# Two gates and the inner values of a linear-attention head: from head columns to token rows, gated before the transposition

## What is computed

```
proj = u @ w_in                  # (hq, hf, hi, hg, gq, gk, gv, ga, gb, gz, gate_h, gate_g)
o_h = hgrn2_chunked(silu(hq)*s, k_h, hi, log_f)           # 8 heads of 128
o_h = rmsnorm(o_h, hgrn_out_norm) * silu(hg)
y_h = o_h @ w_branch_hgrn
o_g = gated_delta_chunked(q_g, k_g, cv, beta, g)          # 16 value heads of 128, 8 key heads
o_g = rmsnorm(o_g, gdn_out_norm) * silu(gz)
y_g = o_g @ w_branch_gdn
y = sigmoid(gate_h) * y_h + sigmoid(gate_g) * y_g         # then y @ w_out
```

## Time and profile before

| | us |
|---|---|
| median of 3 runs | 1413.3 (1413.23 to 1413.37) |
| the profiled execution | 1413.49 |
| its span in the trace | 1411.8 |
| TensorE busy in the span | 1389.9 (98%) |
| VectorE busy | 1042.1 (74%) |
| ScalarE busy | 793.2 (56%) |

### The profile page before, as it was taken

How to read it: one execution, slowest core, us unless ns; L and a number is a source line. 1 busy time by engine, 2 the same in 40 slices (tenths; PEclk the granted TensorE clock), 3 DMA queues, 4 the chain that set the end, 5 groups by cost and what they waited for, 6 DMA issues and landing times.

```text
span 1411.8 us, 26224 instructions
## 1 busy us (share of the span) xinstructions
PE 1389.9 (98%) x9590; PEld 1276.0 (90%) x9590; DVE 1042.1 (74%) x1558; ACT 793.2 (56%) x1275; POOL 28.9 (2%) x73
## 2 busy tenths in 40 slices
PE   8999999999999999999999999999999999999998
PEld 8999999988888878888899999999999898888887
DVE  5786776677666686666798888888888857666665
ACT  4345454644343454444578788788788753544443
POOL 6000000000000000000000000000000000000000
PEclk9999999999999999999999999999999999999999
DMA  8465454565555646566664534534543256556661
GB/s 268 139 179 148 131 138 149 184 206 179 179 191 197 209 140 188 181 196 189 166 165 119 145 96 116 148 98 112 147 104 114 89 155 215 158 180 196 197 199 63
DMA packets 304639, 224.91 MB, mean 159 GB/s; under 512 B 10418, under 2 KB 288068, under 8 KB 304580
## 3 DMA queue, kind: packets, MB, share of 16 engines
q1 hardware_dynamic: 304580, 224.09, 53.7%
HBM read 223.02 MB, written 1.05 MB: 159 GB/s over the span
## 4 chain that ended last, share of the span: by engine, by line
PE 88%; DVE 7%; ACT 2%; DVEq 1%; issue 1%; DMA 0%; ACTq 0%
PE G L1794 10%; PE G L1796 10%; PE G L1795 10%; PE M L1809 7%; PE G L1809 7%; PE M L1799 5%; PE M L1800 5%; PE M L1801 5%; PE G L1811 4%; PE M L1811 4%; PE G L2440 2%; DVE w_lo L1049 2%; PE M L2275 1%; DVEq L1046 1%; PE M L1794 1%; PE G L2442 1%
## 5 line engine op out<-in xcount | busy, mean ns | idle before, releaser
L1049 DVE TENSOR_TENSOR w_lo<-w_raw,w_hi 128x2048 fp32r<-128x2048 f32 (+2 forms) x209 | 475.3, 2277 | 167.6 <-ACT w_hi L575 162.9
L575 ACT ACTIVATE w_hi<-w_raw 128x2048 fp32r<-128x2048 f32 x207 | 394.4, 1907 | 178.9 <-PE G L1796 76.4
L1794 PE MATMUL G<-xa,w_hi 128*128 128x256 f32 x1280 | 382.5, 299 | 0.0
L1796 PE MATMUL G<-xa,w_lo 128*128 128x256 f32 x1280 | 361.9, 283 | 0.0
L1795 PE MATMUL G<-xa,w_hi 128*128 128x256 f32 x1280 | 361.6, 282 | 0.0
L1794 PEld LDWEIGHTS G<-xa,w_hi 128*128 128x128 f32 x1280 | 244.5, 191 | 3.4 <-issue 3.2
L1795 PEld LDWEIGHTS G<-xa,w_hi 128*128 128x128 f32 x1280 | 244.7, 191 | 1.7 <-issue 1.7
L1796 PEld LDWEIGHTS G<-xa,w_lo 128*128 128x128 f32 x1280 | 244.0, 191 | 0.0
L1799 PE MATMUL M<-w_hi,xb 128*128 128x512 f32 x304 | 118.8, 391 | 0.1
L1800 PE MATMUL M<-w_lo,xb 128*128 128x512 f32 x304 | 118.7, 390 | 0.0
L1801 PE MATMUL M<-w_hi,xb 128*128 128x512 f32 x304 | 118.3, 389 | 0.0
(11 more groups left out here) (381 smaller groups left out, 2276.1 us busy)
## 6 DMA issues: line engine op xcount, KB each, us to landing
w_raw<-in_w_in SPq DMA_DIRECT2D x166, 512.0 KB, 4.7
w_raw<-in_ffn_w_in SPq DMA_DIRECT2D x88, 512.0 KB, 5.0
w_raw<-in_w_ff SPq DMA_DIRECT2D x64, 512.0 KB, 4.0
w_raw<-in_ffn_w_out SPq DMA_DIRECT2D x44, 512.0 KB, 4.6
w_raw<-in_w_out SPq DMA_DIRECT2D x16, 512.0 KB, 4.3
w_raw<-in_w_branch_gdn SPq DMA_DIRECT2D x16, 512.0 KB, 5.1
w_raw<-in_w_branch SPq DMA_DIRECT2D x12, 512.0 KB, 4.3
w_raw<-in_w_branch_hgrn SPq DMA_DIRECT2D x8, 512.0 KB, 4.0
```

Of the source, the lines that this page charges most:

```text
L575: nc.scalar.activation(w_hi[:, slot, :], w_raw[:, slot, :], ACT.Copy).then_inc(hi_ready, 1)
L1049: return v.tensor_tensor(dst, src, hi.bitcast(F32), ALU.subtract)
L1794: mm(out_, w[0], x[0], start=first, stop=False)
L1796: return mm(out_, w[1], x[0], start=False, stop=last_)
```

## The change

Chunks 4 and 5 of a head are laid out anew: each holds, for four of the eight k, 512 columns: 128 of hi, 128 of hg, 256 of gz. In their products the tokens are stationary and the weights move (`token_quarter`, with `three_x`), so 48 products of 512 columns take the place of 96 of 256. Tokens 0 to 127 gather in G's bank 1, tokens 128 to 255 in M0, and VectorE and ScalarE copy one each into `tok`. hi needs no transposition any more. One Silu covers hg and gz. The outputs are multiplied with 1/rms and gate by VectorE while tokens are on partitions (`hgrn_gate`, `delta_gate`), then transposed, and ScalarE takes them out with the gain. `level(0)` uses M1 instead of M0, and the transposed matrix M5 instead of M4. In pass 8 the low part of the first four heads' output comes before `scored(0)`, branch products start at place 1, the `WARM` products go, chunks are split in halves, and `delta_turned` follows tile 4.

The core of the diff:

```diff
-EV_Y = (EV_HEADS[0] + 3 * GH, EV_HEADS[1] + 3 * GH)
+EV_Y = (EV_HEADS[0] + 2 * GH, EV_HEADS[1] + 3 * GH)
...
+        def load_tok(c, slot, part, h):
+            slot_free(c)
+            k = slice(4 * part, 4 * part + 4)
+            for at, col in ((0, O_HI), (P, O_HG)):
+                sp.dma_start(rows4(w_raw, slot)[:, :, at:at + P], w_in2[:, k, ds(col + h * P, P)]).then_inc(w_loaded[slot], 16)
+            sp.dma_start(rows4(w_raw, slot)[:, :, T:2 * T], w_in2[:, k, ds(O_GZ + h * CW, CW)]).then_inc(w_loaded[slot], 16)
...
 ScalarE
-            def scaled(out_, o, total, rstd, scale):
+            def token_rstd(out_, o, total, rstd, scale):
...
-                nc.scalar.activation(rstd, rstd, ACT.Exp, scale=-0.5)
-                settle()
-                for x in range(n):
-                    ins = nc.scalar.activation(out_[:, x, :], o[:, x, :], ACT.Copy, scale=rstd[:, x:x + 1])
-                return ins
+                return nc.scalar.activation(rstd, rstd, ACT.Exp, scale=-0.5)
...
+            if not gemm:
+                o_hi(1, 0, 4)
             if main:
                 z_copy(1)
                 y_copy(0)
                 act.wait_ge(gemm_done, c0 + i * 6)
-                nc.scalar.activation(sgz, G[:, 0, :].rearrange("p (e t) -> p e t", e=2), ACT.Copy).then_inc(evac[0], 1)
+                nc.scalar.activation(tok[:, 1, :], M[:, 0, :], ACT.Copy).then_inc(tok_ready, 1)
...
+            if main and gemm:
+                act.wait_ge(hss_done, i)
+                nc.scalar.activation(o_h[:, ds(i - 1, 1), :].rearrange("p n t -> p (n t)"), M[:, 1, T:2 * T], ACT.Copy,
+                                     scale=vec[:, V_HN:V_HN + 1]).then_inc(hfin, 1)
...
 VectorE
+        def delta_gate(i):
+            dve.wait_ge(grs_ready, i)
+            for b in range(TT):
+                for e in range(2):
+                    x, at = 2 * b + e, T + P * e
+                    ins = v.scalar_tensor_tensor(out=zi[:, b, e, :], in0=M[:, 5, P * x:P * x + P], scalar=o_rstd[:, x:x + 1],
+                                                 in1=tok[:, b, at:at + P], op0=ALU.mult, op1=ALU.mult)
+            ins.then_inc(gsq_ready, 1)
...
             decayed(2)
+            if main and gemm:
+                w_low(c0 + 4 + RING - 6, i, 6)
+            if not gemm:
+                o_low(1, 0, 4)
             scored(0)
...
-            w_low_j(3)
             if main and gemm:
-                delta_out(i)
+                delta_gate(i)
...
                 v.drain().then_inc(y0_ready, 1)
+                if main:
+                    delta_out_low(i)
...
                 middle(2)
-            if main and gemm:
-                delta_out_low(i)
+            w_low_j(3)
             if gemm:
-                chunk_done(4)
-                v.tensor_copy(hvt, G[:, 1, 0:T])
-                v.tensor_copy(hsg, G[:, 1, T:2 * T]).then_inc(evac[1], 1)
-                settle()
-            w_low_j(4)
+                dve.wait_ge(tok_done, i + 1)
+                v.tensor_copy(tok[:, 0, :], G[:, 1, :]).then_inc(evac[1], 1)
             settle()
...
 TensorE
-        EARLY = {5: (0, 3), 6: (3, 4), 7: (4, 7), 8: (7, 9), 9: (9, 12), 10: (12, 14), 11: (14, 17), 12: (17, 19),
-                 13: (19, 21), 14: (21, 25), 15: (25, 28)}
-        WARM = {1: 1, 2: 2, 3: 2, 4: 2}
+        EARLY = {1: (0, 2), 2: (2, 3), 3: (3, 5), 4: (5, 6), 5: (6, 8), 7: (8, 10), 8: (10, 11), 9: (11, 13), 10: (13, 14),
+                 11: (14, 17), 12: (17, 19), 13: (19, 21), 14: (21, 25), 15: (25, 28)}
+            def token_quarter(n):
+                part, b, k0 = n // 4, n % 4 // 2, 2 * (n % 2)
+                if n % 4 == 0:
+                    weights_ready(c0 + 4 + part + i * 6)
+                if n == 0:
+                    pe.wait_ge(evac[1], EV_HEADS[1] + 2 + i * 3)
+                wh, wl = rows4(w_hi, (c0 + 4 + part) % RING), rows4(w_lo, (c0 + 4 + part) % RING)
+                blk = slice(P * b, P * b + P)
+                for k in range(k0, k0 + 2):
+                    x = 4 * part + k
+                    ins = three_x(G[:, 1, :] if b == 0 else M[:, 0, :], (xa_hi[:, x, blk], xa_lo[:, x, blk]),
+                                  (wh[:, k, :], wl[:, k, :]), x == 0, x == KT - 1)
+                if n % 4 == 3:
+                    ins.then_inc(gemm_done, 1)
+                if n == 5:
+                    ins.then_inc(tok_done, 1)
...
-            if gemm:
-                pe.wait_ge(evac[1], EV_HEADS[1] + 3 + i * 3)
-                for b in range(TT):
-                    ins = nc.tensor.transpose(M[:, 1, P * b:P * b + P], hvt[:, P * b:P * b + P], ident[:])
-                ins.then_inc(hvt_done, 1)
```

More of the change, by code:

```diff
@@ L192, in emit @@
     sct = mix(3 * P)
[L193 to L196, removed]
+    hrs = mix(T)
     raw = grid(mix(4 * (T + 4)), n=4, t=T + 4)
@@ L351, in small_cols, with loads, rows4 @@
         return cols(ring, 0)[:, :, 0:P + SMALL]
+    def loads(c):
+        tok_chunks = [FIRST["heads"] + 6 * h + j for h in range(GH) for j in (4, 5)]
+        third = sum(1 for n in tok_chunks if n <= c and n % RING == c % RING)
+        return 32 * (c // RING + 1) + (16 if c % RING == 0 else 0) + 16 * third
+    def rows4(ring, slot):
+        return ring[:, slot, :].rearrange("p (k c) -> p k c", c=512)
     def rows2(ring, slot):
@@ L567, in split @@
                 return
-            act.wait_ge(w_loaded[slot], 32 * (base // RING + 1) + (16 if slot == 0 else 0) + i * (32 * step // RING))
+            act.wait_ge(w_loaded[slot], loads(base) + i * (loads(base + step) - loads(base)))
             if base >= RING:
@@ L575, in split, with split_half @@
                 nc.scalar.activation(w_hi[:, slot, :], w_raw[:, slot, :], ACT.Copy).then_inc(hi_ready, 1)
+        def split_half(c, h):
+            slot = c % RING
+            act.wait_ge(w_loaded[slot], loads(c))
+            act.wait_ge(gemm_done, c - RING + 1)
+            part = slice(CHUNK // 2 * h, CHUNK // 2 * (h + 1))
+            ins = nc.scalar.activation(w_hi[:, slot, part], w_raw[:, slot, part], ACT.Copy)
+            if h == 1:
+                ins.then_inc(hi_ready, 1)
         def x_hi(n):
@@ L924, in head @@
                 o_hi(2, 4, GH - 1)
+                split_half(FIRST["yh"] + 2, 1)
             compact(3)
@@ L1654, in head @@
                 ins.then_inc(vn0_ready, 1)
+            if not gemm:
+                w_low_half(FIRST["yh"] + 2, 0)
             if gemm:
@@ L1664, in head @@
                                 ).then_inc(r1_ready, 1)
+            if not gemm:
+                hgrn_gate(i)
+                w_low_half(FIRST["yh"] + 2, 1)
             if gemm:
@@ L1673, in head @@
                 if not gemm:
-                    hgrn_out()
-                    o_low(3, GH - 1, GH)
+                    dve.wait_ge(ohh_ready, 3)
+                    gain_low(xa_lo[:, GH - 1, :], M[:, 1, T:2 * T], V_HN, xa_hi[:, GH - 1, :]).then_inc(ohl_ready, 1)
+                    delta_gate(i)
+                else:
+                    hgrn_gate(i)
             if gemm:
@@ L2250, in level @@
                     blk = slice(P * b, P * b + P)
-                    ins = mm(M[:, 0, blk], left[:, blk], right[:, blk], start=True, stop=True)
+                    ins = mm(M[:, 1, blk], left[:, blk], right[:, blk], start=True, stop=True)
                 ins.then_inc(lev_done, 1)
@@ L2429, in _ @@
             yh_part(tile, GH - 1 if tile < 4 else 0, GH)
-            if tile == 3:
+            if tile == 4:
                 delta_turned(GH)
```

107 lines of the change are left out of this document (52 added, 55 removed).

## The result

| | median us | lowest to highest | profiled execution | its span |
|---|---|---|---|---|
| before | 1413.26 | 1413.14 to 1413.37 | 1413.49 | 1411.8 |
| changed | 1429.74 | 1429.14 to 1430.75 | 1429.88 | 1428.2 |

The changed kernel takes 1.0117 of the time before (95% interval 1.0100 to 1.0135): it is slower by 16.5 us. The forecast was 1424.9 with a range of 1417 to 1432. So direction and range held, and the forecast was 4.8 us too low. Most of what follows is about two questions: whether the named cause is the true one, and where the 4.8 us are.

The account below looks back on a forecast made before the run. VectorE's slackless work between `kq_done` and `inverse(1)` was taken to set each head. Heads +10.9, eighth head +0.2, tail +0.5 sum to +11.6 us: 1424.9 us against 1413.3, range 1417 to 1432.

Parts of the forecast that it names:

- VectorE's stretch: VectorE's work from `kq_done` to `inverse(1)`, said to have no slack: 10.83 us before, 12.78 after, +1.95 a head.
- the end of 0.5 us a head: Other end for `delta_gate` coming late at TensorE's transpositions: cover 0.2 us, nothing taken in the forecast.
- first period: From `kq_done` of pass 0 to the next: +1.26 us at `inv_z(2)`, +0.97 at the next `kq_done`.
- six more periods: Full heads: 52.59 + 1.95 - 0.29 = 54.25 us each, +1.66 a head, 9.96 in six.
- eighth head, to the first product behind it: Head 8: VectorE's longer work costs about 0.9 us at `inv_z(2)`, 0.7 comes back, +0.2 where the chain ends.
- tail, to the first product of the next stage: Behind head 8: tile 4 starts as before at about 1139.9, four transpositions of some 0.4 us come on top: +0.5.
- I give these 0.7 us: Head 8's inverse levels: gain from dropping seven warm-up products and halving a late w_lo of 2.2 us.
- rival 3: Slower still, 1430.9 us: `delta_gate` late, 3.5 us, and clock falling in head 8, 2 to 3; 0.14 with Rival 4.
- The form's saving: TensorE's rows: 512-column products save 0.58 us a head, two dropped `hvt` transpositions 0.22; only 0.29 was counted.
- Rival 1: VectorE's work does not set the head, TensorE's savings all count: faster, 1401 to 1407 us; chance 0.12.
- Rival 2: Head 8 pays back 5 to 6 us through earlier fill and dropped warm-up products: 1418.7 us; chance 0.13.
- Rival 4: The tokens' form misses the pace, so the 0.29 saving is nil: +2.3 us; chance 0.14 with rival 3.

Follow-up runs that it names:

- experiment 1: Changed kernel with `w_low_j(3)` put ahead of VectorE's wait for `kq_done` instead of behind `middle(2)`: 1414.8 us.
- experiment 4: Kernel before with only `w_low_j(3)` moved behind `middle(2)`, nothing of the new form, gates or eighth head: 1432.31 us.
- experiment 5: Changed kernel with three warm-up products in the eighth head, ahead of quarter 1's wait: 1428.66 us.
- experiment 9: Kernel before with chunk 1's low part moved behind `middle(3)` and chunk 2's behind `middle(6)`: 1413.44 us.
- experiment 3: Changed kernel with `w_low_j(3)` ahead of the `kq_done` wait and low parts of chunks 1 and 2 behind `middle(3)` and `middle(6)`: 1411.01 us.
- experiment 6: Changed kernel with the last head's `delta_gate` behind the two products that empty tiles 0 and 1 of the branch product: 1426.06 us.
- experiment 2: Changed kernel with only the low parts of chunks 1 and 2 moved, behind `middle(3)` and `middle(6)`: 1425.06 us.
- experiment 7: Changed kernel, eighth head: three warm-up products, low part of four heads' output behind `middle(3)`, fill from quarter 2: 1427.88 us.
- experiment 8: Changed kernel with all low-part moves, last `delta_gate` later; eighth head: output's low part behind `middle(3)`, one warm-up product, ScalarE's high part behind `y_copy(0)`: 1407.26 us.

## Why the prediction was right, and where 4.8 us are

**The mechanism held, step by step.** VectorE's stretch: forecast 12.78 us, measured 12.94. Wait ahead of quarter 0: 1.6, measured 1.62 to 1.64 in the full heads (0.74 in head 1, which has no `delta_out_low` in its stretch). Wait ahead of `inv_z(2)`: 0.9, measured 0.77. VectorE's stand before `kq_done`: some 2 us, measured 1.87 (0.84 in pass 0). Copy out of G: 0.69, measured 0.68. No wait ahead of the transpositions behind quarter 18: `delta_gate` was in time, and the end of 0.5 us a head was not touched. DMAs: no wait on them in the heads. Experiments 1 and 4 show the cause in both directions.

**The sum, by place**, from the two profiled executions, one of each kernel:

| place | forecast | measured |
|---|---|---|
| first product of the first projection (10.30 to 10.99) | 0 | +0.69 |
| from there to `kq_done` of pass 0 | -0.29 | -0.25 |
| first period | +1.26 | +1.12 |
| six more periods | 6 x 1.66 = +9.96 | 6 x 1.905 = +11.43 |
| eighth head, to the first product behind it | +0.2 | +1.34 |
| tail, to the first product of the next stage | +0.5 | +2.10 |
| sum | +11.6 | +16.4 |

The terms that were mis-sized:

- *The period*, 0.25 us in each of six heads. Of it 0.16 is in the sum 2.07 + 0.66 + ...: in front of `delta_out_low` VectorE stands 0.35 us ("issue") behind the copy with its drain, where in the steps that I added up from the earlier trace rows only 0.12 stood behind that copy. A step read elsewhere does not carry the gap that it will have behind a new neighbour. The other 0.09 lies behind `inv_z(2)`: from there to the next `kq_done` it takes 41.09 us for 41.29, so 0.20 is saved and not 0.29.
- *The eighth head*. The stretch came out at +1.08 at `inv_z(2)` for 0.9. From there to the first product behind the head it takes 26.13 us for 25.87 before: +0.26, where "I give these 0.7 us" had -0.7. The clock makes the difference. In experiment 5, where it did not fall, the same way takes 25.15 us, so -0.72. The 0.7 us held, and the fall's 1.0 us was missing from the sum.
- *The tail*. Tile 4 started 0.22 us later than before, relative to the first product behind the head; the forecast was 0. The four transpositions were 0.36 for 0.4. What was missing is the clock behind the wait of 2.29 us: products of 256 columns at 0.21 us and not 0.12 over 3.3 us, some 1.4 us. I had put it at 2 to 3 us in rival 3 and kept it out of the sum, with the waits of 1.36 and 1.66 us before as the argument. The Trainium skill, "TensorE: Matmul & The Clock Gate", section "Why this matters for your kernels", warns of idle gaps between bursts of products, and of longer ones than these; the trace agrees with the direction of that warning, not with the length.
- *The beginning*, +0.69. No edit touches it. Over all eleven profiled executions, of kernels whose code is the same up to there, that product starts between 10.07 and 10.99 us; the changed kernel's profiled one is the latest. It is no effect of the change.

**The form's saving.** The forecast was 0.58 + 0.22 = 0.80 us a head if TensorE sets the time. The kernels to compare are those of experiments 9 and 3, which have the same moves: 0.53 us in a full head (52.57 less 52.03). Up to `inv_z(2)` it is 0.30 (11.08 less 10.78) for a forecast of 0.51, and behind it 0.24 for 0.29. What is missing in the first part, 0.2 us, I can't place; the pace itself, 0.229 us in the new rows, is right. Against the kernel before, experiment 3 gains nothing behind `inv_z(2)` (41.26 us for 41.29). There the moved low part of chunk 2 costs it 0.2, as in experiment 9: `inverse(3)` ends at 1011.96, and `inv_z(4)` starts 0.05 later, 4.39 us behind `inv_z(3)` for 4.20 before.

```profile
1007.62 0.62 PE L2328 MATMUL M<-arena 128*128 128x128 f32 x4
...
1012.01 0.71 PE L2328 MATMUL M<-arena 128*128 128x128 f32 x4
```

So the moves took VectorE off one place where TensorE waits for it and put it, by 0.2 us, on another.

**The rivals.** Rival 1 (the stretch does not set the head) is refuted by experiments 1 and 4. Rival 2 (the eighth head pays 5 to 6 us back) did not happen: earlier fill gives nothing while `inverse(1)` and ScalarE's copies come when they come. Rival 3 was half right: the clock, not `delta_gate`. Rival 4 falls with the pace, which is 0.229 in the new rows too: (1115.10 - 1113.04) / 9.

## What to carry to other kernels

Before moving a step on an engine that isn't the bottleneck, look at the interval between two hand-overs in which it lands. This change took 2.2 us out of a place where VectorE would wait and put them between a release and the work that TensorE waits for next; the same step in the same kernel, some twenty lines further up, gives 14.9 of the 16.5 us back. Where VectorE stands for less time, as in the first pass, even that place makes TensorE wait 0.7 us. Where an interval has two exits (here a bank that is emptied and a matrix that is updated), shortening it behind the first one gives only the difference. And when fill products are taken out of a stretch with waits, price the clock for what follows, not only the products.

## What the runs showed of the hardware

The granted clock fell behind waits of TensorE that differ little from waits that left it alone. With 1.10 and 1.43 us of waiting and 0.7 us of work between, it fell to 0.50 in three kernels, for 3.4 us (changed, experiment 6) and 6.5 us (experiment 2). With 1.27 and 0.22 us (experiments 1 and 3) it stayed at 1.00, and so it did with 1.11 us and three products of no use behind it (experiment 5). Such products are no guarantee: experiment 4 has those of the kernel before, its waits there are 1.67, 0.48 and 1.55 us, and the clock fell for 2.9 us; in the kernel before, with 0.48 and 1.36 us, it did not. The single wait of 2.29 us ahead of tile 4 brought it down in the changed kernel and in experiments 2, 3, 5 and 7, and not in the profiled execution of experiment 1, where the windows before and behind show 1.00 throughout:

```profile
1135.00:1140.00 5.00, 2.71 (x24) 2.54 (x23) 1.93 (x7) 3.78 (x12) 0.00 (x0) 1.00 0.75 210
1140.00:1145.00 5.00, 5.00 (x44) 5.00 (x44) 5.00 (x4) 2.16 (x2) 0.00 (x0) 1.00 0.27 80
```

So the same wait does not always bring the clock down, and the fall cost some 1.4 us in the changed kernel. That would make the time scatter, but that it parts the two groups of experiment 1 is not shown. They are 2 us apart, at mean clocks of 0.999 and of 0.996 to 0.999, and only one execution has a trace. The ten executions of experiment 3, which has the same wait, form no such groups (1410.64 to 1411.64), and the kernel before, without it, ranges from 1413.14 to 1415.68 on that chip. The four executions of experiment 8, in which no TensorE wait from the eighth head on is longer than 0.6 us, lie within 0.5 us.
